# Branch chunk split within attention, results ahead of low halves in drains, high halves two places ahead

## The reference

```
h = rms_norm(x, norm_mix)
q, k, v of three mixers, merge_gate = split(h @ w_in)
o_a, o_b, o_c = nsa_attention(...), banded_attention(...), moba_attention(...)
y = einsum('bsmc,mcd->bsmd', stack([o_a, o_b, o_c]), w_branch)
x = x + sum(sigmoid(merge_gate) * y, axis=2) @ w_out
x = x + square(relu(rms_norm(x, norm_mlp) @ w_mlp_in)) @ w_mlp_out
```

```
s1 = softmax(q1 @ k1.T * scale); s2 = softmax(q2 @ k2.T * scale)     # mixer A
o = (s1 - lam * s2) @ v
y = concat([y1, y2]) * silu(ug)
x = x + gate * (y @ w_o[l])
```

## Time and profile before

| | |
|---|---|
| median of 3 runs | 2984.72 us (2983.91 to 2986.87) |
| profiled execution | 2982.89 us |
| its span | 2981.1 us, 37294 instructions |
| PE busy | 2936.4 us (99%) |
| DVE busy | 1924.8 us (65%) |
| ACT busy | 1266.2 us (42%) |
| POOL busy | 217.6 us (7%) |

### The profile page before, as it was taken

How to read it: one execution, slowest core, us unless ns; L and a number is a source line. 1 busy time by engine, 2 the same in 40 slices (tenths; PEclk the granted TensorE clock), 3 DMA queues, 4 the chain that set the end, 5 groups by cost and what they waited for, 6 DMA issues and landing times.

```text
span 2981.1 us, 37294 instructions
## 1 busy us (share of the span) xinstructions
PE 2936.4 (99%) x14159; PEld 2403.4 (81%) x14159; DVE 1924.8 (65%) x2700; ACT 1266.2 (42%) x2045; POOL 217.6 (7%) x308
## 2 busy tenths in 40 slices
PE   8999999999999999999999999999999999999998
PEld 7897788878888888888887877777888887877877
DVE  5886466668868888888865734454544534666655
ACT  5443354543444444443555223333333324435444
POOL 1000000011001010010100000000000100102000
PEclk9999999999999999999999999999999999999999
DMA  8987956568768878878865733333343624776444
GB/s 271 299 296 270 311 177 189 149 194 279 260 211 267 275 265 275 269 261 275 268 205 172 246 126 113 117 113 121 107 134 121 217 87 141 246 237 202 138 134 160
DMA packets 315426, 611.09 MB, mean 205 GB/s; under 512 B 29373, under 2 KB 90010, under 8 KB 314352
## 3 DMA queue, kind: packets, MB, share of 16 engines
q1 hardware_dynamic: 296012, 544.74, 56.5%
q0 software_dynamic: 18272, 62.64, 6.0%
q10 hardware_dynamic: 964, 1.33, 0.2%
HBM read 567.94 MB, written 41.85 MB: 205 GB/s over the span
## 4 chain that ended last, share of the span: by engine, by line
PE 93%; DVE 3%; ACT 1%; issue 1%; DMA 0%; SPq 0%; POOL 0%; POOLq 0%; ACTq 0%; DVEq 0%
PE acc L686 28%; PE acc L688 27%; PE acc L687 27%; PE acc L1507 3%; PE acc L1477 2%; PE acc L1495 2%; DVE w_lo L508 1%; PE acc L1067 1%; PE acc L1475 1%; PE acc L1455 1%; ACT w_hi L502 1%; PE acc L715 1%; PE acc L781 0%; DMA raw<-in_w_in 0%; PE acc L616 0%
## 5 line engine op out<-in xcount | busy, mean ns | idle before, releaser
L686 PE MATMUL acc<-w_hi,a_hi 128*128 128x512 f32 (+3 forms) x3736 | 1483.0, 397 | 10.3 <-DVE w_lo L508 6.8
L688 PE MATMUL acc<-w_hi,a_lo 128*128 128x512 f32 (+3 forms) x3736 | 1448.2, 388 | 0.0
L687 PE MATMUL acc<-w_lo,a_hi 128*128 128x512 f32 (+3 forms) x3736 | 1446.6, 387 | 0.0
L508 DVE TENSOR_TENSOR w_lo<-raw,w_hi 128x1024 fp32r<-128x1024 f32 (+3 forms) x778 | 932.6, 1212 | 384.4 <-ACT w_hi L502 378.8
L502 ACT ACTIVATE w_hi<-raw 128x1024 fp32r<-128x1024 f32 (+3 forms) x778 | 805.4, 1047 | 731.3 <-PE acc L688 671.3
L686 PEld LDWEIGHTS acc<-w_hi,a_hi 128*128 128x128 f32 x3736 | 703.5, 188 | 167.7 <-issue 21.5
L688 PEld LDWEIGHTS acc<-w_hi,a_lo 128*128 128x128 f32 x3736 | 702.6, 188 | 142.7
L687 PEld LDWEIGHTS acc<-w_lo,a_hi 128*128 128x128 f32 x3736 | 704.2, 188 | 126.6
L545 DVE SCALAR_TENSOR_TENSOR lanes_b<-raw,ct,lanes_b 128x1024 f32<-128x1024 f32 x150 | 189.5, 1304 | 0.0
L545 DVE SCALAR_TENSOR_TENSOR lanes_c<-raw,ct,lanes_c 128x1024 f32<-128x1024 f32 x120 | 156.7, 1348 | 0.0
L1553 ACT ACTIVATE pb<-acc,at_st 128x256 f32<-128x256 f32 (+4 forms) x144 | 71.1, 494 | 139.8 <-DVE at_st L1665 91.8
(11 more groups left out here) (431 smaller groups left out, 1767.8 us busy)
## 6 DMA issues: line engine op xcount, KB each, us to landing
raw<-in_w_mod SPq DMA_DIRECT2D x192, 512.0 KB, 4.8
raw<-in_w_in SPq DMA_DIRECT2D x128, 512.0 KB, 5.0
raw<-in_w_mlp_in SPq DMA_DIRECT2D x128, 512.0 KB, 4.4
raw<-in_w_mlp_out SPq DMA_DIRECT2D x128, 512.0 KB, 5.4
raw<-in_e_w_in SPq DMA_DIRECT2D x104, 512.0 KB, 4.4
raw<-in_w_o SPq DMA_DIRECT2D x64, 512.0 KB, 5.0
raw<-in_o_w_in SPq DMA_DIRECT2D x64, 512.0 KB, 4.8
raw<-in_w_in SPq DMA_DIRECT2D x56, 448.0 KB, 4.6
```

The source lines that it names most:

```text
L508: nc.vector.tensor_tensor(w_lo[:, n % SPLITS, 0:size], raw[:, r % RAWS, 0:size], w_hi[:, n % SPLITS, 0:size].bitcast(F32), ALU.subtract)\
L686: nc.tensor.matmul(o, s.lhs(0, kt, tt), wh, start=kt == 0 and not s.goes_on, stop=False)
L687: nc.tensor.matmul(o, s.lhs(0, kt, tt), wl, start=False, stop=False)
L688: last = nc.tensor.matmul(o, s.lhs(1, kt, tt), wh, start=False, stop=end)
```

## The change

It has three parts.

1. The run of the first region is made longer by `branch`. Its first chunk now gets its high half in the last but one place of the region and its low half in the last.
2. The result becomes a function of its own. For pairs it stands between `join` and `lo` instead of behind both. In a drain the result of unit u-3 comes in place u itself, behind `silu` and ahead of `lo`, the turned activations and the parts; the loop is one place shorter.
3. The high half of a chunk stands two places ahead of its first pair in passes of pairs too (one before). The low half stays one place ahead.

```diff
-        for run in (("qkv0", "qkv", "qkv_end", "gates_a", "gates_b", "gates_c"),
+        for run in (("qkv0", "qkv", "qkv_end", "gates_a", "gates_b", "gates_c", "branch"),
                     ("branch", "out1", "mlp", "in2", "in2_rest", "out2"),
...
-                    big = where[first[x] - 1][0][0].pairs
-                    hi = max(first[x] - (1 if big else 2), free, -1)
+                    hi = max(first[x] - 2, free, -1)
...
+            def result(self, dve, link, p, i):
+
+                if i == 0 and p.saves0:
+                    dve.wait_ge(at_saved, 16 * p.saves0)
+                w, v = p.units[i], p.u0 + i
+                st = at_st[:, v % 8, :]
+                dve.wait_ge(o_done, v + 1)
+                if w.add:
+                    dve.wait_ge(e_done, v)
...
-                    for u in range(p.U + 4):
-                        if u == 4 and p.saves0:
-                            dve.wait_ge(at_saved, 16 * p.saves0)
+                    for u in range(p.U + 3):
                         if 0 <= u - 1 < p.U and p.units[u - 1].pair:
                             self.join(dve, link, p, u - 1)
+                        if 4 <= u <= p.U:
+                            self.result(dve, link, p, u - 4)
+                        if 0 <= u - 1 < p.U and p.units[u - 1].pair:
                             self.lo(dve, p, u - 1)
-                        if 0 <= u - 4 < p.U:
-                            w, v = p.units[u - 4], p.u0 + u - 4
...
-                        if u <= p.U + 2:
-                            self.silu(dve, p, u)
-                            if u >= p.U or not p.units[u].pair:
-                                self.lo(dve, p, u)
-                            for feed, x in p.turns.get(u, ()):
-                                feed.lo(dve, x)
+                        self.silu(dve, p, u)
+                        if u >= p.U:
+                            self.result(dve, link, p, u - 3)
+                        if u >= p.U or not p.units[u].pair:
+                            self.lo(dve, p, u)
+                        for feed, x in p.turns.get(u, ()):
+                            feed.lo(dve, x)
```

More of the change, by code:

```diff
@@ L1582, in join @@
                                                op0=ALU.mult, op1=ALU.add).then_inc(pair_done, 1)
+            def result(self, dve, link, p, i):
[6 more added lines that the diff above has]
+                    dve.wait_ge(e_done, v)
+                if w.sink is not None and p.guard:
+                    link(nc.vector.tensor_scalar(st[:, 1:2], st[:, 1:2], st[:, 2:3], TINY,
+                                                 ALU.add, ALU.max))
+                elif w.sink is not None:
+                    link(nc.vector.tensor_tensor(st[:, 1:2], st[:, 1:2], st[:, 2:3], ALU.add))
+                elif p.guard:
+                    link(nc.vector.tensor_scalar(st[:, 1:2], st[:, 1:2], TINY, None, ALU.max))
+                link(nc.vector.reciprocal(st[:, 3:4], st[:, 1:2]))
+                if w.coeff is not None and not w.pair:
+                    link(nc.vector.tensor_tensor(st[:, 3:4], st[:, 3:4], w.coeff, ALU.mult))
+                o = acc[:, self.obanks[v % len(self.obanks)], 0:P]
+                if w.add:
+                    nc.vector.scalar_tensor_tensor(out=w.out, in0=o, scalar=st[:, 3:4], in1=w.out,
+                                                   op0=ALU.mult, op1=ALU.add).then_inc(e_done, 1)
+                elif w.gate is not None:
+                    if i == 0 and p.kept:
+                        for bank, _ in p.kept.tiles:
+                            dve.wait_ge(acc_free[bank], p.kept.fill[bank] + 1)
+                    elif i == 0:
+                        dve.wait_ge(gate_there, 16 * p.gates_end)
+                    if i == 0:
+                        for feed, x in p.turned_first:
+                            feed.turned(dve, x)
+                    nc.vector.scalar_tensor_tensor(out=w.out, in0=o, scalar=st[:, 3:4], in1=w.gate,
+                                                   op0=ALU.mult, op1=ALU.mult).then_inc(e_done, 1)
+                else:
+                    nc.vector.tensor_scalar(w.out, o, st[:, 3:4], None, ALU.mult)\
+                      .then_inc(e_done, 1)
             def dve(self, dve):
```

## The result

| | before | after |
|---|---|---|
| median | 2983.61 us (6 runs) | 2997.23 us (6 runs, 2994.85 to 2999.16) |
| ratio | | 1.0044 (95% interval 1.0034 to 1.0055) |
| span of the profiled execution | 2981.1 us | 2993.9 us |

The change makes the kernel 13.6 us slower. The page after answers the earlier trace rows: PE's busy time is the same within 1.6 us, and the span is 12.8 us longer, so PE stands idle more.

A forecast was written before the change was run, and what follows sets the result against it. TensorE, busy 99% of the span, bounds the kernel, so only its idle or slow-clock time counts. Losses of 21.95 us less gains of 7.85 give +14.1 us, 2998.8 us (0.47% slower), range 2989 to 3004.

The forecast's parts named there:

- the wait of 5.3 us behind the rope: Mixer A, second to third pass: rope and low half follow the last result, PE idles 5.3 us; 6.6 us lost with clock.
- one of 3.3 us a pass later: Mixer A, third to fourth pass: rope and low half outlast six pairs, idle 3.45 us; 5.15 us lost with clock.
- the smaller ones at the ends named: Other pass ends: losses of 3.3 (fourth to fifth), 2.2 (first region), 1.65 (D) and 3.05 us together for the rest.
- the rival of the cover: Ends of passes: PE has enough work to cover rope and low half, only gains remain, 2976.9 us; chance 0.05.
- The clock's rule: Gaps on PE: above 3 us charged 1.7 us more than their length, 2 us or less only their length.
- The branch step: First chunk of the branch step: halves made earlier, 1.7 us of wait saved and 1.7 us of clock, 3.4 us gained.
- The edits for pairs: A pass of mixer A around 2003 to 2012: result first, 1.6 us of wait saved, with clock 3.3 us gained.
- My 0 for the other units: Other 31 units of mixer A: no output waits, earlier result and high half change nothing on PE, 0 us.
- The drains' gain: Second pass of mixer D: result one place earlier lets PE's output start sooner, 1.15 us gained.
- the low half of D's first to second pass: Mixer D, first to second pass: low half ready later behind the last result, PE's fill starts late, 1.65 us lost.
- That half is given back: Ends of passes: DVE and ACT run ahead while PE is late, losses halve to 11 us, 2987.9 us; chance 0.12.
- The clock rival: Clock behind gaps: holds over 3.45 and 5.3 us, 2995.4 us, chance 0.1; or falls at three more, 3003.9 us, chance 0.18.

The follow-up runs named there:

- The probe: Kernel with the last result put back, plus 0 to 3 extra subtractions ahead of 64 MLP low halves to make gaps on PE; 3223.69 us (one run).
- The kernel without gaps over 1.2 us: Changed kernel with only each pass's last result put back behind the low half, turned activations and parts of its place; 2972.35 us, 0.9967 of the kernel before.

## Why the prediction was right, point by point

**The mechanism and its places were right.** PE's waits after show the wait of 5.3 us behind the rope, one of 3.3 us a pass later and the smaller ones at the ends named. In the table above eleven of the thirteen terms came within 0.25 us, and the 13.6 us of the medians lie beside a forecast of 14.1. The walk, DVE's queue put in its new order with the durations of before and PE's pairs laid beside it, needed no other information. One reading of the rows was wrong without consequence: between the last output and the chunk at 1842.05 PE has three pairs and a wait of 0.41 us, not four pairs. The term used the old start of that chunk, so the count did not enter it; it stands only in the rival of the cover. The experiments show that the drains make the loss, the last result of each pass nearly all of it, and the lost cover of rope and low half is how.

**The clock's rule was wrong.** I charged 1.7 us behind a gap above 3 us and nothing at 2 us or less. The gap of 3.29 us lost nothing and that of 1.96 us in the first region lost 1.7. The two errors cancelled (5.15 against 3.6, and 2.2 against 3.9). The probe shows that this was luck: gaps of 1.8 to 2.2 us lose half the time, gaps of 3.1 to 3.6 us lose eight times in eleven. A forecast should have carried a share of 1.7 us for each: for the gaps of 5.32, 3.29 and 1.96 us of the changed kernel (1, 8 in 11 and 1 in 2) that is 3.8 us where I charged 3.4, with a wider range. The Trainium skill, TensorE: Matmul & The Clock Gate, section "What's actually happening", calls the activity window free-running. By that, gaps of one length can end differently, and the probe's trace agrees (2.12 us lost 1.7 us of work, 2.11 lost none).

**The branch step.** 3.4 us forecast and measured. That the clock came back behind the 1.57 us that are left is what all 21 probe gaps of up to 1.74 us do. The part alone gains more (4.3 us at the place), since in the changed kernel the early last result stands ahead of the low half.

**The edits for pairs.** 3.3 us at the place, as forecast, but I took ACT's copy `pt` for a part of the cause; the run with the result alone shows that the output does not need it. My 0 for the other units holds: no new wait appears there. That the earlier high half changes nothing on PE was wrong at one chunk, the one at 1842.05, where the high half was the late one: there it gives 0.7 us by itself. In the changed kernel the rope stands ahead of that chunk's low half and hides this.

**The drains' gain** was 1.2 us, as forecast (1.15), the low half of D's first to second pass 1.4 and not 1.65, a term a little mis-sized.

**The rivals.** That the cover is enough fell at the place it named: three pairs, where eleven were needed. That half is given back did not come true: each place kept its loss up to the end of the trace, and the waits of before that could have vanished are small (6.8 us in all). The clock rival was real in both directions, and within one kernel.

## What to carry to other kernels

An instruction that waits for another engine's *last* output is a fence in its own queue: before it is moved ahead, list what stands behind it and what of that ran beside the other engine until now. Moving a short step forward in all places of a loop can gain at the inner places and lose at the end; here putting back one of them per pass turned +13.6 us into -10.9. In these kernels gaps on TensorE of 1.8 us and more had an additional price in some cases and not in others, so a schedule that keeps all of them under 1.7 us is worth more than the sum of its gaps.

## What the runs showed of the hardware

Behind the probe's gaps the clock fell to 0.50 (1.2 GHz) in none of 21 cases up to 1.74 us, and in all four of 4.76 us. In between it was open: the gap of 3.36 us ahead of the branch step, same instructions up to there, cost 1.7 us of work in the kernel before and in those of the result and of the high half alone, and nothing in the kernel with both edits for pairs. The gap of 3.17 us in mixer A cost 1.7 us before and 3.0 us with the branch chunk alone. The gap of 1.96 us in mixer D cost nothing in four kernels and 1.7 us with the result alone, and the one of 1.96 us in the first region cost 1.7 us in the changed kernel and nothing with the drains alone. Where the fall came while PE still waited, as at 1846.54 with its 5.3 us, part of the slow stretch was spent idle and cost nothing. The kernel without gaps over 1.2 us had no clock loss in its trace. Whether that also makes its runs agree better (2971.49 to 2974.32 in 5 runs, against 2980.52 to 2985.98 in 21 of the kernel before) stays open with so few.
